# Hybrid decoder block: input units in pieces between the attention's steps, and the rest of the mixer reordered around them

## The reference

```
mod = silu(c) @ w_ada + b_ada;  sh1, sc1, gt1, sh2, sc2, gt2 = split(mod, 6)
h = rms_norm(x, g_pre_mix) * (1 + sc1) + sh1
hq, hf, hi, hgate, pv, aq, ak, av = split(h @ w_in)      # w_in: 1024 x 2048
o_a = hgrn2_mixer(hq, hf, hi, hgate, ...)   # gated recurrence, 4 heads, 256 channels
o_b = pool_mixer(pv, pool_w, pool_scale)    # causal means over 2, 4, 8, 16 tokens, minus pv
o_c = sink_swa_attention(aq, ak, av, sinks) # 8 heads, 2 kv heads, window 128
x = x + gt1 * rms_norm(concat(o_a, o_b, o_c) @ w_out, g_post_mix)
h = rms_norm(x, g_pre_ffn) * (1 + sc2) + sh2
x = x + gt2 * rms_norm(conv_ffn(h, ...), g_post_ffn)   # w_up 1024 x 5632, w_down 2816 x 1024
```

## Time and profile before

| what | us |
|---|---|
| median of three runs | 2425.37 |
| the profiled execution | 2425.92 |
| its span in the trace | 2424.1 |
| PE busy with matmuls | 2307.9 (95% of the span) |
| DVE busy | 1228.4 (51%) |
| ACT busy | 769.6 (32%) |
| POOL busy | 300.1 (12%) |
| share of PE in the chain that ended last | 86% |
| share of DVE, ACT, issue in that chain | 6%, 3%, 2% |

### The profile page before, as it was taken

One profiled execution on the slowest core, in us unless ns is written; L12 is line 12 of the kernel. 1 busy time (PEld: TensorE's weight loads), 2 busy tenths in 40 slices (PEclk: granted clock), 3 DMA queues, 4 the chain that ended last, 5 costly groups with the idle time before them and its releaser, 6 DMA issues.

```text
span 2424.1 us, 33058 instructions
## 1 busy us (share of the span) xinstructions
PE 2307.9 (95%) x11307; PEld 1856.9 (77%) x11307; DVE 1228.4 (51%) x2073; ACT 769.6 (32%) x1500; POOL 300.1 (12%) x219
## 2 busy tenths in 40 slices
PE   6997799999999899999999899999999989999997
PEld 4775678788788578888888767888887857888886
DVE  3347277484855735244454646425254574515345
ACT  3435343333432632112133344112133263211212
POOL 2322234444403000000001100000000300000000
PEclk9998999999999899999999999999999999999999
DMA  9961468888664135655555324655546414555555
GB/s 352 380 239 74 156 215 306 294 296 284 217 263 154 53 139 208 225 191 191 192 191 192 138 88 171 228 191 190 191 165 236 157 53 158 222 209 191 191 191 191
DMA packets 115399, 483.16 MB, mean 199 GB/s; under 512 B 8000, under 2 KB 38986, under 8 KB 69706
## 3 DMA queue, kind: packets, MB, share of 16 engines
q1 hardware_dynamic: 115273, 481.53, 54.7%
HBM read 378.74 MB, written 102.76 MB: 199 GB/s over the span
## 4 chain that ended last, share of the span: by engine, by line
PE 86%; DVE 6%; ACT 3%; issue 2%; DMA 1%; SPq 1%; DVEq 0%; ACTq 0%
PE ps L633 17%; PE ps L635 17%; PE ps L634 17%; PE ps L649 8%; PE ps L650 8%; PE ps L651 8%; PE ps L712 2%; ACT SM L1186 1%; PE ps L678 1%; PE ps L800 1%; PE ps L764 1%; DVE SM L1537 1%; DMA raw<-in_w_in_dram 1%; SPq L281 1%; DVE hTl L1459 1%
## 5 line engine op out<-in xcount | busy, mean ns | idle before, releaser
L633 PE MATMUL ps<-hTh,wt 128*128 128x512 f32 x1920 | 753.8, 393 | 8.9 <-DVE hTl L1459 5.1
L634 PE MATMUL ps<-hTl,wt 128*128 128x512 f32 x1920 | 749.0, 390 | 0.0
L635 PE MATMUL ps<-hTh,wt 128*128 128x512 f32 x1920 | 748.9, 390 | 0.0
L633 PEld LDWEIGHTS ps<-hTh,wt 128*128 128x128 f32 x1920 | 361.7, 188 | 92.4 <-issue 15.2
L635 PEld LDWEIGHTS ps<-hTh,wt 128*128 128x128 f32 x1920 | 361.4, 188 | 76.3
L634 PEld LDWEIGHTS ps<-hTl,wt 128*128 128x128 f32 x1920 | 361.6, 188 | 73.7
L1673 DVE TENSOR_SCALAR cv<-ub,CW 128x512 f32<-128x512 f32 x176 | 99.9, 568 | 473.2 <-ACT ub L1304 457.2
L1304 ACT ACTIVATE ub<-ps 128x512 f32<-128x512 f32 x176 | 105.3, 598 | 691.6 <-PE ps L635 677.1
L649 PE MATMUL ps<-wt,pTh 128*128 128x512 f32 x704 | 277.7, 394 | 1.8 <-ACT T L1075 1.8
L650 PE MATMUL ps<-wt,pTl 128*128 128x512 f32 x704 | 277.3, 394 | 0.0
L651 PE MATMUL ps<-wt,pTh 128*128 128x512 f32 x704 | 274.7, 390 | 0.0
(11 more groups left out here) (237 smaller groups left out, 2493.5 us busy)
## 6 DMA issues: line engine op xcount, KB each, us to landing
wt<-split_w SPq DMA_DIRECT2D x268, 1024.0 KB, 4.8
split_w<-wt SPq DMA_DIRECT2D x88, 1024.0 KB, 7.1
raw<-in_w_up_dram SPq DMA_DIRECT2D x22, 1024.0 KB, 9.6
XT<-in_w_ada_dram SPq DMA_DIRECT2D x11, 1024.0 KB, 8.2
XN<-in_x_dram SPq DMA_DIRECT2D x5, 2048.0 KB, 9.6
raw<-in_w_in_dram SPq DMA_DIRECT2D x8, 1024.0 KB, 13.8
XT<-in_x_dram SPq DMA_DIRECT2D x4, 2048.0 KB, 9.3
raw<-in_w_down_dram SPq DMA_DIRECT2D x8, 1024.0 KB, 9.3
```

The source lines that it names most:

```text
L633: mm(ps[:, bank, :], w, hTh[:, k, :], start=(k == 0), stop=False)
L634: mm(ps[:, bank, :], w, hTl[:, k, :], start=False, stop=False)
L635: ins = mm(ps[:, bank, :], wl[:, slot, k, :], hTh[:, k, :], start=False, stop=(k == KD - 1))
```

## The change

In neutral words, by part:

1. **Units 12 to 15 in pieces.** `FILL` cuts the last four input units into runs of two to four k tiles, which stand on PE between the parts of the attention: two k tiles of unit 12 before `scores(0)` and six after `scores(1)`, four of unit 13 after the recurrence, and then one piece in each of the eight steps. All four use PSUM bank 7.
2. **Which columns a unit holds.** `IN_PAIRS` swaps the pooling's and the gate's pairs: units 8 and 9 are now the gate, 10 to 13 the queries, 14 and 15 the pooling's values.
3. **Levels earlier.** `level(0)` and `level(1)` stand behind unit 6, and the others behind units 7, 8, 9, 10; `level(6)` stands after `scores(0)`. The chunk states' product comes right after `level(5)`. Token transposes stand inside units 6, 8 and 10.
4. **The attention's order.** Steps go by kv head first (heads 0 to 3 for all four token tiles, then heads 4 to 7). `scores` runs two steps ahead in each step, and the value product runs one step behind. The result goes to a buffer `ATT` over `XT` instead of into `hTh` and `hTl`, and the output product takes its channel pairs in another order (`OUT_K`).
5. **Pooling.** Its window sums move from POOL to DVE (`window_sums`, one half in step 6, one half after the last step), and its matmul moves behind the second output unit.
6. **x in its own place.** The residual's x is loaded into `XR`, over the buffers of the probabilities, and that load waits for the last value product (`pv_mm`). The output stays in `XT`.
7. **Block 0.** The sets of `mod` stand behind units 0, 2, 3, 5, 7, 8, 9, 10 (before: every second unit, 0 to 14); their columns stand inside the next unit; DVE's 16 diagonal instructions move into step 2.

```diff
-IN_PAIRS = (2, 0, 4, 14, 8, 10, 12, 6)
+IN_PAIRS = (2, 0, 4, 14, 6, 10, 12, 8)
-OUT_K = ((2, 3), (0, 1), (4, 5), (6, 7))
+OUT_K = ((4, 5), (6, 7), (0, 1), (2, 3))
-ADA_AFTER = {2 * i: 4 + i for i in range(8)}
+ADA_AFTER = {0: 4, 2: 5, 3: 6, 5: 7, 7: 8, 8: 9, 9: 10, 10: 11}
+FILL_BANK = 7
+FILL = {0: (13, 4, 8), 1: (14, 0, 2), 2: (14, 2, 5), 3: (14, 5, 8), 4: (15, 0, 2), 5: (15, 2, 4), 6: (15, 4, 6), 7: (15, 6, 8)}
...
             def load_x(b):
-                sp.wait_ge(s["out_stored"], b * 64 + 64)
...
-                sp.dma_start(XT[:], x_d[ds(b * BT, BT), :]...
+                sp.wait_ge(s["pv_mm"], b * 8 + 8)
+                sp.dma_start(XR[:], x_d[ds(b * BT, BT), :]...
...
+                unit(6, {3: tokens_v})
+                level(0, 2)
+                level(1, 2)
+                unit(7)
+                level(2, 2)
+                unit(8, {3: tokens_va})
+                level(3, 3)
+                unit(9)
+                level(4, 3)
+                unit(10, {1: tokens_k, 5: tokens_g})
+                level(5, 7)
+                chunk_states()
+                unit(11)
+                k_tiles(12, 0, 2)
+                pe.wait_ge(s["acc_taken"], eb_ + 12)
+                pe.wait_ge(s["k_copied"], b * 4 + 4)
+                scores(0)
+                pe.wait_ge(s["state_ready"], b * 8 + 8)
+                level(6, 7)
...
+                scores(1)
+                k_tiles(12, 2, KD)
...
+                fenced(s["level_taken"], b * 13 + 13)
+                recurrence()
+                k_tiles(13, 0, 4)
+                for x_ in range(8):
+                    if x_ == 2:
+                        pe.wait_ge(s["acc_taken"], eb_ + 14)
+                    if x_ + 2 < 8:
+                        scores(x_ + 2)
+                    transposed_probs(x_)
+                    if x_:
+                        weighted_values(x_ - 1)
+                    k_tiles(*FILL[x_])
+                weighted_values(7)
...
                 for u in range(1, U_OUT - 2):
+                    if u == 2:
+                        pe.wait_ge(s["acc_taken"], eb_ + E_IN)
+                        pooling()
...
+                def window_sums(a):
+                    dve.wait_ge(s["acc_taken"], eb_ + 15 + a)
+                    step(ts(PV[:, a, 0:16], PVc[:, a, :], 1.0, None, ALU.mult))
+                    cur, nxt = (y[:].rearrange("p a n -> p (a n)")[:, 0:E_] for y in (Q, K))
+                    x_ = PV[:, a, :]
+                    step(tt(cur[:, 1:], x_[:, 1:], x_[:, 0:E_ - 1], ALU.add))
+                    for n, w in enumerate((2, 4, 8)[:3 if a else 1]):
+                        r = slice(64, 128) if n == 2 * a else slice(0, 128)
+                        step(tt(nxt[r, 2 * w - 1:], cur[r, 2 * w - 1:], cur[r, w - 1:E_ - w], ALU.add))
+                        cur, nxt = nxt, cur
...
-                    stt(XT[:, t, :], XN[:, t, :], rs[:, 1, t:t + 1], XT[:, t, :], ALU.mult, ALU.add).then_inc(s["fin_done"], 1)
+                    stt(XT[:, t, :], XN[:, t, :], rs[:, 1, t:t + 1], XR[:, t, :], ALU.mult, ALU.add).then_inc(s["fin_done"], 1)
```

More of the change, by code:

```diff
@@ L500, in low @@
                 pool.tensor_tensor(lo, src, hi.bitcast(fp32), ALU.subtract).then_inc(s["w_lo"], 1)
-            n_pre = step.n
             pool.wait_ge(s["w_lo"], RING)
[L504 to L547, removed]
@@ L549, in _ @@
-            one_block(0, True)
-            with pool.Fori(1, NB) as b:
-                one_block(b, False)
+            for u in range(RING, OFF_UP[0]):
+                pool.wait_ge(s["unit_done"], u - RING + 1)
+                low(0, u)
+            for f in range(3):
+                with pool.Fori(0, FH[f] // 2) as i:
+                    for u in range(4):
+                        pool.wait_ge(s["unit_done"], i * 4 + (OFF_UP[f] + u - RING + 1))
+                        low(i * 4, OFF_UP[f] + u)
+                for u in range(KD):
+                    pool.wait_ge(s["unit_done"], OFF_DN[f] + u - RING + 1)
+                    low(0, OFF_DN[f] + u)
@@ L637, in k_tile, with mixed, hidden, product_tm @@
                         ins.then_inc(s["unit_done"], 1)
-                def product_tm(u, n, ks, ph, hi, lo, first, last, bank_free=None):
+                def mixed(k, t):
+                    if k >= 4:
+                        return ATT[:, t, 0, k - 4, :], ATT[:, t, 1, k - 4, :]
+                    return hTh[:, k, t * P:t * P + P], hTl[:, k, t * P:t * P + P]
+                def hidden(k, t):
+                    return pTh[:, k, t * P:t * P + P], pTl[:, k, t * P:t * P + P]
+                def product_tm(u, n, ks, ph, parts, first, last, bank_free=None):
                     flat = lambda w, j: w[:, u % RING, :, :].rearrange("p k n -> p (k n)")[:, j * 512:j * 512 + 512]
@@ L646, in product_tm @@
                         for j, k in enumerate(ks):
-                            h, l = (y[:, k, t * P:t * P + P] for y in (hi, lo))
+                            h, l = parts(k, t)
                             f, e = first and j == 0, last and j == len(ks) - 1
@@ L724, in one_block @@
                     pe.wait_ge(s["stage_taken"], 3)
[L725 to L752, removed]
                 def scores(x_):
-                    t, hh = x_ // 2, x_ % 2
+                    t, hh = x_ % 4, x_ // 4
                     if x_ >= 2:
@@ new lines, in tokens_g @@
+                def tokens_g():
+                    pe.wait_ge(s["acc_taken"], eb_ + 10)
+                    token_major((5, 6), [two_tiles(UT, 0, g) for g in range(2)])
+                for u in range(6):
+                    if u < 4:
+                        pe.wait_ge(s["y_added"], b * 16 + (u + 1))
+                    unit(u)
+                pe.wait_ge(s["y_added"], b * 16 + 8)
+                unit(6, {3: tokens_v})
+                level(0, 2)
+                level(1, 2)
+                unit(7)
@@ L1113, in one_block @@
                 act.activation(QE[:], QE[:], ACT.Exp).then_inc(s["q_exp"], 1)
-                for u in (4, 5):
-                    done(u)
-                    take(u, UT[:, u - 4, :])
-                    refill_in(u)
+                done(4)
+                take(4, UT[:, 0, :])
+                refill_in(4)
                 act.wait_ge(s["b_ready"], b * 2 + 2)
@@ L1231, in one_block @@
                        .then_inc(s["o_squared"], 1)
-                att_high(0)
-                for x_ in range(1, 8):
+                act.wait_ge(s["out_stored"], b * 64 + 64)
+                for x_ in range(8):
+                    if x_ == 1:
+                        done(13)
+                        take(13, AQ[:, 3, :])
+                        refill_in(13)
                     probs_copy(x_)
+                    if x_:
+                        att_high(x_ - 1)
                     if x_ + 2 < 8:
                         exps(x_ + 2)
-                    att_high(x_)
-                    if x_ == 5:
+                    if x_ == 2:
                         act.wait_ge(s["oss_ready"], b + 1)
@@ L1614, in one_block @@
                             .then_inc(s["o_ready"], 1)
-                if first:
-                    dve.wait_ge(s["mod_read"], ADA_SETS - ADA_PRE)
-                    pre_(tt(MOD[:, 16:48], MOD[:, 16:48], VT[:, 16:48], ALU.add))
-                    diagonals(0)
-                    scale_and_shift(1)
-                    diagonals(1)
+                    if x_ == 6:
+                        window_sums(0)
+                att_low(7)
+                for a in range(2):
+                    split(a, a)
+                window_sums(1)
+                step(ts(corr[:].rearrange("p a n -> p (a n)"), ones[:, 0:32], 1.0, None, ALU.mult))
+                step(ts(PVc[:], PV[:, :, BT:BT + 16], 1.0, None, ALU.mult))
                 n_pre = pre_.n
-                for a in range(2):
-                    split(2 + a, a)
                 step(V.tensor_copy(SS[:, 0, :, :], SS[:, NC, :, :]))
@@ L1628, in one_block @@
                 step(V.tensor_copy(bmask[:, 1, :, :], bmask[:, 0, :, :]))
+                for a in range(2):
+                    split(2 + a, 2 + a)
                 def tile_done(ph, n, t):
```

321 lines of the change are left out of this document (172 added, 149 removed).

## The result

The changed kernel takes 2387.6 us (median of 4 runs, 2383.1 to 2391.5) against 2422.0 of the kernel before beside it: ratio 0.9855, 95% interval 0.9825 to 0.9884. It is faster by 34 us, not by 72; 2354 was too low, and 2387.6 lies above the range. Rivals B and C gave 2386 each. That is the number and not the reason: B is not what happened, as the waits show, and of C only a small part is. The profiled execution is the fastest of the four, so the two traces differ by more than the medians: span 2424.1 less 2381.4 is 42.7 us.

The account below looks back on a forecast made before the run. PE, busy 95% of the span, was taken as the bound, losing time to waits and a low clock. Stretches 70 us plus block 0's output 5.8, less 4 for handoffs, gave 72 off 2425.9: 2354, range 2341 to 2382.

Parts of the forecast that it names:

- B: Rival: in the attention's steps, handoffs between engines pace PE, 1 us waited in each of 32 steps: 2386 us, chance 0.12.
- C: Rival: the clock still falls in the attention, for whatever reason, losing 32 us of the gain: 2386 us, chance 0.07.
- The sum of PE's work: PE's work from unit 5's end to the first output matmul, added at 2.4 GHz with cuts: 107.4 us.
- The levels: Between units 6 to 10 and after: PE passes one level every 7.26 us, rounds take 6.3 to 6.8, not waited for.
- E: Rival: the levels' chain stands in series with the units, 4.4 us at 24 places, 105 us: 2459 us, chance 0.06.
- That most of the clock comes back: Sign: PEclk 0.99 or more in the stretch from unit 5's end to the first output matmul.
- The charge of 2 us for block 0's output weights: Block 0's output weight pairs load behind x, so ACT stops ahead of the pooled channels' copies: 0 to 5 us, taken 2.
- D: Rival: block 0's output weight pairs load behind one another instead of pipelined, 12 us late: 2366 us, chance 0.05.
- Steps: PE needs: Attention steps: PE needs 4.9 to 5.6 us each, the whole round of some 7 us has 10, so no waits.
- 55.8 - 5.8 + 1.9: Block 0's output units: 55.8 us before, 5.8 saved after charges, pooling's 1.9 added.
- The 4 us for handoffs: Allowance for unseen handoffs of 0.2 to 0.3 us: 1 us a block, 4 in all, taken off the gain.
- the walk's 71.6 us: Gain in four blocks' stretches by summing PE's work; waits plus clock gave 65.9, and 70 was taken.

Follow-up runs that it names:

- a_take: Changed kernel with ScalarE's copy of unit 14 issued ahead of step 4's copy of the transposed probabilities: 2371.8 us, 0.977 of the kernel before.
- a_align: Changed kernel with 32 unused bytes behind nwcol, restoring the later tiles' places modulo 64: 2373.9 us, 0.9786 of the kernel before.
- b_shift: Kernel before with an unused tile of 32 bytes behind wcol, nothing else: ratio 1.0052.
- c_pad32: a_both with 32 unused bytes ahead of pTh, moving only it and the FFN's tiles behind it: 2371.0 us, 0.9764 of the kernel before.
- c_cols: a_both with the columns of mod's set 4 in block 0 behind seven of unit 1's k tiles instead of two: 2350.5 us, 0.968 of the kernel before.
- c_pad128: a_both with 128 unused bytes ahead of pTh: 0.9757 of the kernel before.
- c_pad448: a_both with 448 unused bytes ahead of pTh: 0.9722 of the kernel before.
- a_both: Changed kernel with both 32 unused bytes behind nwcol and ScalarE's earlier copy of unit 14: 2356.0 us, 0.971 of the kernel before.
- c_whole: a_both with units 13 to 15 run whole between the recurrence and step 0, no pieces between steps: 2388.8 us, 0.984 of the kernel before.
- b_64: Kernel before with 64 unused bytes behind wcol: ratio 0.9987.
- c_pad64: a_both with 64 unused bytes ahead of pTh: 2368.7 us, 0.9756 of the kernel before.

## Why the prediction was wrong

Right, by its own steps:
- The sum of PE's work. 107.4 us was forecast for the stretch; 110.5 less the 2.89 of the wait is 107.6 in block 1. Pooling at 1.9 us in the output units too: 45.39 for 45.7 forecast.
- The levels. No wait on them is in the trace, in any block, so E falls. So does, as put, B (one wait of 0.97 us in 32 steps).
- That most of the clock comes back: 0.65 in the window of block 1 is gone, the stretch has 1.00 (0.99 and 0.98 in the others).

- The charge of 2 us for block 0's output weights, in place of the 12 us of D. ScalarE stands 14.14 us for the first pair; the pooled channels' copies and their splits come behind it, and PE waits 0.78 us for the one and, ahead of output unit 3, 2.62 for the other. The splits were slow besides: a cast and a subtraction of 0.42 and 0.69 us took 1.18 and 2.71 beside a POOL instruction (block 0, 242.9 to 246.8 us).

```profile
240.21 2.01 ACT L989 ACTIVATE wt<-raw 128x1024 fp32r<-128x1024 f32 x2 [14.14 <-DMA raw<-in_w_out_dram]
...
248.03 0.47 PE L631 MATMUL ps<-wt,hTh 128*128 128x512 f32 x1 [2.62 <-DVE hTl L1469]
```

Wrong:
1. **"Steps: PE needs ... ACT had 22.3 us in the 30 us ... and three steps get a 0.60 copy. Not waited for."** This is the step that failed. I counted ScalarE's busy time per step and not the place of the copy in its program, nor that unit 15 needs the bank which that copy frees. 12.2 us of waits, and about 4 us of clock behind them (a_take: 15.8). In a small way this is C, as the trace shows a fall behind the 3.5 us wait of block 0 and behind a 2.9 us wait in two of the three later blocks; but it is a consequence of the wait. What I held against C, that all falls came behind a gap of 3.4 us or more, was misread. Blocks 2 and 3 of the kernel before have a second fall each: in block 2 the clock is 1.00 from 1381.2 to 1384.5 us and 0.50 from 1384.7 to 1387.9, behind a wait of 2.66 us.

```profile
1384.70 1.03 PE L760 MATMUL ps<-bmask,identb 128*128 128x512 bf16 x2 [2.66 <-ACT st L1189]
```

2. **The FFN, which the sum carried over unchanged.** 6.9 us between the two traces, 9.3 by the pace alone, by 32 bytes (a_align, b_shift, c_pad32). No row of the trace before could give it; the diff's new tile was in sight, its effect was not.
3. **Block 0: its start and its output.** The stretch begins 5.5 us later (95.70 instead of 90.18), of which 3.3 is the longer wait for G's copy (c_cols); the rest is PE's clock and the DMAs' arrival, which differ from run to run there, and was not tested. The stretch took 128.6 us for 120.6 forecast: 3.5 and 0.97 of waits, 1.5 of clock, some 2 that I can't place. The output units came to 53.8 with pooling, 1.9 more than forecast (55.8 - 5.8 + 1.9): the two waits above are 3.4 us where 2 were charged. No run changes them.
4. The 4 us for handoffs that I didn't see were not needed, and the walk's 71.6 us had been taken as 70.

Between the two spans: the four stretches came out 8.0, 3.1, 4.7 and 4.7 us above the sum, together 20.4 (12.2 of waits, about 4.5 of clock behind them in blocks 0, 2 and 3, and 3.0 more in block 0). With 6.9 for the FFNs, 5.5 for the start and 1.9 for block 0's output, less 4 and 1.6, that is 29.1, for the 29.3 that are missing (72 less 42.7). Between the medians 38 are missing; the further 9 is the spread of the runs, the profiled one of the changed kernel being its fastest and that of before above its median.

With the copy moved, the FFN's operands at a good place and the columns later, c_cols takes 2350.5 us against 2425.6: 75 us, of which some 4.6 is the better place of pTh than before's (2112 x 0.0022). The rest, 70, is near the 72 of the forecast.

## What to carry to other kernels

When work is threaded between steps, walk the program of the engine that drains it, not its busy share: a copy of 0.6 us on an engine that is half idle cost 2.9 us of PE in each block, since it stood behind instructions that waited for PE's next step. Two units in one PSUM bank make each such copy a point of order.

A sum for the changed part carries the rest of the kernel over as it is; where a change adds or resizes a tile, compare the addresses of the matmuls' operands before and after, and look at the spacing of starts in a stretch that the change doesn't touch.

## What the runs showed of the hardware

The pace of a gapless run of fp32r matmuls (128 columns stationary, 512 moving) depends, in these runs, on where the tiles from pTh on begin in a partition of SBUF; pTh and pTl are the stationary operands of the matmuls that change their pace. With every slice of pTh and pTl a multiple of 512 bytes from the tile's start, and the moving tile at remainder 128, the means over 192 gapless starts are, the same in each block to 0.0001:

| start of pTh, remainder to 512 | kernels | us a start |
|---|---|---|
| 0 | c_pad128 | 0.2324 |
| 320 | before, c_pad448 | 0.2289 |
| 352 | changed, a_take, b_shift | 0.2333 |
| 384 | a_align, a_both, c_cols, c_whole, b_64 | 0.2267 |
| 416 | c_pad32 | 0.2333 |
| 448 | c_pad64 | 0.2333 |

hTh, at remainder 128, goes at 0.227 in the output units of the kernel before, the changed one and a_align alike. The whole effect is 2.9% of a matmul, 14 us of this kernel.

The tiles behind pTh (pTl, Y, ub, cv, P32) moved with it, and ScalarE and VectorE work on them. But the pace isn't set by their work: in the changed kernel 981 down products with no instruction of VectorE, ScalarE or GpSimd under way come at 0.2333 us and 1097 beside one at 0.2333 too. The six places also have six different remainders to 256 (0, 64, 96, 128, 160 and 192), and hTh at 128 goes like pTh at 384, so no run tells a period of 256 bytes from one of 512. Why is not shown; whether the moving operand's place counts, and whether pTh's or pTl's place matters more, was not tried.

The clock can fall behind a PE gap of 2.9 us or not: in the changed kernel it did in blocks 2 and 3 (0.98 in the stretch) and not in block 1 (1.00), for the same instructions in the same order. With PE busy 24.0 of 30 us in short gaps, the longest 2.2 us, it stayed at 1.00 (c_whole, 790 to 820 us), with nothing but transposes, scores and value products up to 819.2 us. The Trainium skill ("TensorE: Matmul & The Clock Gate", "Part 4: PE-mode transpose") has full clock not engaging in transpose mode; in these steps, where full clock was already there, it was kept. This is a cleaner case than the 30 us that the prediction took from rows 2, which begin with the pooling's four 512-column products; the clock rose at 817.9 us, while they ran:

```profile
815.63 3.09 PE L789 MATMUL ps<-R,PW 128*128 128x512 f32 x4
```
